# Key pages of a paged cache turned three steps ahead on VectorE, in a one-layer hybrid decoder step

## The reference

```python
q, k, v, g_a, u, v_n, g_b, m_a, m_b = split(rmsnorm(x) @ w_in)     # one projection, 5632 columns
attn = moba(q, k, v)          # prompt: causal, blocks of 256;  sample: over the cache
sgu  = u * (tril(w_s) @ v_n + b_s)                                 # chunks of 128, by group
mixed = sigmoid(m_a) * (attn * silu(g_a)) @ w_pa + sigmoid(m_b) * (sgu * silu(g_b)) @ w_pb
y = rmsnorm(x + mixed @ w_o)
# moba of the sample, for each sample, head and new position:
gate = q . mean(k over each block of 256 cached positions)         # 8 blocks
sel  = the 3 blocks with the largest gate
p    = softmax(q k / 8 + position bias, over the selected blocks and the new positions)
out  = p v
```

## Time and profile before

| | |
|---|---|
| median of 3 runs | 547.55 us (544.87 to 548.51) |
| profiled execution | 548.5 us, its span 546.7 us |
| TensorE matmuls busy | 519.2 us, 95% |
| VectorE busy | 307.8 us, 56% |
| ScalarE busy | 179.7 us, 33% |
| GpSimd busy | 121.2 us, 22% |
| granted clock of TensorE, mean | 0.986 |
| DMA | 112.00 MB, mean 205 GB/s |

### The profile page before, as it was taken

One profiled execution on the slowest core, in us unless ns is written; L12 is line 12 of the kernel. 1 busy time (PEld: TensorE's weight loads), 2 busy tenths in 40 slices (PEclk: granted clock), 3 DMA queues, 4 the chain that ended last, 5 costly groups with the idle time before them and its releaser, 6 DMA issues.

```text
span 546.7 us, 13830 instructions
## 1 busy us (share of the span) xinstructions
PE 519.2 (95%) x5624; PEld 474.6 (87%) x5624; DVE 307.8 (56%) x686; ACT 179.7 (33%) x389; POOL 121.2 (22%) x108
## 2 busy tenths in 40 slices
PE   8999999999999999999979689989979999999993
PEld 6999999989899999998979689879978999998672
DVE  6624333476765655766833767985433454784524
ACT  5522222233433432454442241212151141343313
POOL 1201111331411411321231235422360300000002
PEclk9999999999999999999999999989997999999998
DMA  8645533377648778677498998877798792360004
GB/s 253 183 155 169 182 119 119 103 229 250 195 153 272 224 252 292 200 237 247 145 334 259 302 306 285 252 245 220 255 308 292 228 330 79 126 230 1 2 10 153
DMA packets 73561, 112.00 MB, mean 205 GB/s; under 512 B 5501, under 2 KB 35338, under 8 KB 73498
## 3 DMA queue, kind: packets, MB, share of 16 engines
q1 hardware_dynamic: 72122, 107.51, 60.4%
q0 software_dynamic: 1232, 3.36, 2.1%
q10 hardware_dynamic: 144, 0.26, 0.1%
HBM read 106.57 MB, written 4.53 MB: 203 GB/s over the span
## 4 chain that ended last, share of the span: by engine, by line
PE 78%; DVE 8%; DMA 7%; SPq 3%; issue 2%; ACT 0%; POOL 0%; POOLq 0%; DVEq 0%; ACTq 0%
PE BK L583 36%; PE BK L603 9%; PE BK L922 8%; DMA KRAW<-in_cache_k 7%; PE BK L737 4%; PE BK L751 4%; PE BK L672 2%; DVE KT L1332 2%; PE BK L799 2%; PE BK L816 2%; PE BK L617 2%; PE BK L806 2%; SPq L511 1%; PE BK L852 1%; PE BK L779 1%
## 5 line engine op out<-in xcount | busy, mean ns | idle before, releaser
L583 PE MATMUL BK<-XH,WH 128*128 128x272 f32 x672 | 202.9, 302 | 0.0
L583 PE MATMUL BK<-XL,WH 128*128 128x272 f32 x672 | 194.5, 289 | 0.0
L583 PE MATMUL BK<-XH,WL 128*128 128x272 f32 x672 | 194.5, 289 | 0.0
L583 PEld LDWEIGHTS BK<-XH,WH 128*128 128x128 f32 x672 | 127.8, 190 | 10.8 <-issue 10.0
L583 PEld LDWEIGHTS BK<-XL,WH 128*128 128x128 f32 x672 | 127.7, 190 | 0.0
L583 PEld LDWEIGHTS BK<-XH,WL 128*128 128x128 f32 x672 | 127.4, 190 | 0.0
L1695 POOL TENSOR_TENSOR WL<-WRAW,WH 128x1024 fp32r<-128x1024 f32 x32 | 76.7, 2396 | 207.9 <-ACT WH L971 207.9
L1332 DVE STREAM_TRANSPOSE KT<-KRAW 128x512 f32<-128x512 f32 x128 | 87.9, 699 | 55.1 <-DMA KRAW<-in_cache_k 54.6
L971 ACT ACTIVATE WH<-WRAW 128x1024 fp32r<-128x1024 f32 x52 | 55.0, 1057 | 15.6 <-PE BK L603 15.6
L737 PE MATMUL BK<-KT,QW 128*32 128x128 f32 x1024 | 35.0, 278 | 15.5 <-DVE KT L1332 15.5
L737 PEld LDWEIGHTS BK<-KT,QW 128*32 128x32 f32 x1024 | 26.2, 110 | 20.8 <-DVE KT L1332 17.0
(11 more groups left out here) (207 smaller groups left out, 810.5 us busy)
## 6 DMA issues: line engine op xcount, KB each, us to landing
KRAW<-in_cache_k SPq DMA_DIRECT2D x128, 256.0 KB, 4.6
WRAW<-in_w_in SPq DMA_DIRECT2D x21, 1024.0 KB, 7.8
VRAW<-in_cache_v SPq DMA_DIRECT2D x56, 256.0 KB, 3.5
VQT<-in_cache_v SPq DMA_DIRECT2D x28, 256.0 KB, 4.1
VEX<-in_cache_v SPq DMA_DIRECT2D x24, 256.0 KB, 3.8
VGU<-in_cache_v SPq DMA_DIRECT2D x20, 256.0 KB, 3.7
WO<-in_w_o SPq DMA_DIRECT2D x4, 1024.0 KB, 6.3
XR<-in_x_prompt SPq DMA_DIRECT2D x4, 512.0 KB, 4.9
```

Source lines behind the costliest of these rows:

```text
L583: last = mm(BK[h][:, 0:HALF], w[:, n % 2, k, :], x[:, k, cols], start=(i == 0 and w is WH and x is XA), stop=(i == KC - 1 and w is WL))
```

## The change

VectorE turns two pages in each of the steps 0, 1 and 2, and from step 3 on page t+3 in step t; SyncE asks for page i+4 in the step in which page i is turned, as before, so its requests move along. The group x = 2 of a sample's scores used to come after `page_sums` of the groups 0 and 1 by the order of turns; it now waits for them by a semaphore of its own, `rh_ok`.

```diff
+AHEAD = 3
+def turned_at(t):
+    return [i for i in ((2 * t, 2 * t + 1) if t < AHEAD else (t + AHEAD,)) if i < PAGES]
...
 # SyncE
             for t in range(STEPS):
-                if t + KR < PAGES:
-                    load_k(t + KR)
+                for i in turned_at(t):
+                    if i + KR < PAGES:
+                        load_k(i + KR)
...
 # TensorE, page_scores
                     wait(pe, pt_ok, b - 1)
+                if x == 2:
+                    pe.wait_ge(rh_ok, b + 1)
                 for k in range(4):
...
 # VectorE, page_sums
                 peak = dve.tensor_reduce(KP[:, 4 * x:4 * x + 4], sc, AX.XY, ALU.max)
-                if x == 1:
+                if x == 0:
+                    peak.then_inc(rh_ok, 1)
+                else:
                     link(peak)
...
 # VectorE, the steps
                 if t == 0:
                     rows_out(N_QKV - 1)
-                if t < PAGES:
-                    page_turn(t)
+                for i in turned_at(t):
+                    page_turn(i)
                 if t % 4 == 0 and 4 <= t <= 128:
```

More of the change, by code:

```diff
@@ L410, in build @@
         kt_ok, sc_pe, qr_pe, qr_ok, qw_ok, bw_ok = sem("kt_ok"), sem("sc_pe"), sem("qr_pe"), sem("qr_ok"), sem("qw_ok"), sem("bw_ok")
-        r_ok, gm_pe, gm_ev, eb_ok, ex_ok = sem("r_ok"), sem("gm_pe"), sem("gm_ev"), sem("eb_ok"), sem("ex_ok")
+        rh_ok, r_ok, gm_pe, gm_ev, eb_ok, ex_ok = sem("rh_ok"), sem("r_ok"), sem("gm_pe"), sem("gm_ev"), sem("eb_ok"), sem("ex_ok")
         pt_pe, pt_ok, pl_ok, lm_pe, rl_ok = sem("pt_pe"), sem("pt_ok"), sem("pl_ok"), sem("lm_pe"), sem("rl_ok")
```

## The result

The changed kernel takes 544.15 us (median of 20 runs, 541.56 to 546.29), the kernel before 547.94 us beside it; the ratio is 0.9932, interval 0.9912 to 0.9952, or 3.8 us less. The forecast was 7.5 us less, so half of the gain is missing. The profiled execution took 545.19 us (span 543.4 us, mean granted clock 0.981).

A forecast was written before the change was run, and what follows sets the result against it. TensorE, busy 95% of the span, was taken as the bound, so only its waits for VectorE could return. Terms 3.4 - 5.3 - 3.3 + 0 + 0 - 4.6 + 2.3 = -7.5 us: profiled 541.0, median 540.0; range 532 to 548.

The forecast's parts named there:

- bank 0 at the start: Step 2: the turns of pages 4 and 5 delay the silu that frees bank 0; TensorE waits +3.4 us.
- waits of VectorE's order, and that of 3.49: Page-score waits of 1.70, 2.66 and two small ones go, -5.3 us; that of 3.49 at step 120, -3.3 us.
- waits of 3.00 and 3.67 move to the gate sums: Steps 72 and 80: these waits become one of 7.5 us for R at step 82; net 0 us.
- new waits elsewhere: Turns waiting for earlier page scores, and rh_ok at step 16b+12: taken at 0, from 0 to +2 us.
- old clock losses: After the waits at 357.25 and 411.24: 1.7 and 2.9 us lost at lower clock go, -4.6 us.
- clock behind the two new waits: After the new waits of 3.4 and 7.5 us: lower clock costs +2.3 us, between 0 and 5.8.
- each is charged the mean over the four: Each new wait costs 1.15 us of clock, the mean of 1.7, 2.9, 0 and 0 after four old waits.
- The second: Clock falls at both new waits and step 120's 3.3 us come only in half: 545 us, chance 0.27.
- its other half: Step 120: the 3.3 us come only in half, +1.7 us in the second rival, chance 0.27.
- the forecast's 536 to 545: 540.0 us with the lower and upper bounds of the start and new clock losses; chance 0.45.
- The first rival: SyncE's stretch from 287.89 moves up, so all waits go and 6.7 us come back: 532 us, chance 0.15.
- The third: VectorE stands for landings ahead of work TensorE needs at each handover; slower, 555 us, chance 0.13.

The follow-up runs named there:

- second profile: The changed kernel run again unchanged for a second profile: 542.17 us.
- the second one of before: The kernel before run again unchanged for a second profile: 550.37 us.
- the three later groups: The follow-up experiments, each group on another chip, in which the kernel before took 549.01, 550.37 and 549.11 us.
- The test with products in the waits: Changed kernel with unread products on TensorE, 7 before the wait for bank 0 and 14 before that for R: 0.9868 to the kernel before, 543.37 us.
- the lead grown late with and without the constants: Changed kernel with lead one up to step 67, three from step 70: 0.9865 to the kernel before; with constant loads also at step 80: 0.986.
- the silu moved: Changed kernel with VectorE's silu of step 2 ahead of that step's two page turns: 0.9908 to the kernel before.

## Why the prediction was half right

Term by term, on the profiled execution:

| step | forecast, us | measured, us |
|---|---|---|
| bank 0 at the start | 3.4 | 3.29, second profile 3.20 |
| waits of VectorE's order, and that of 3.49 | go | L747 waits for no turn |
| waits of 3.00 and 3.67 move to the gate sums | 7.5 | 7.21, second profile 6.57 |
| new waits elsewhere | 0 (0 to 2) | 1.23 (L809), second profile 1.35 (a bank behind ScalarE) |
| old clock losses | -4.6 | those places at 1.00 |
| clock behind the two new waits | 2.3 | 4.2 |

**The waits.** Before, L737 and L765 waited 16.9 us, and L806 0.2. The forecast takes 3.4 - 5.3 - 3.3 = -5.2 to that and so leaves 11.9; the profile has 7.8 + 3.3 + 1.2 + 0.3 = 12.6, the second one 12.5. These steps held to within 0.7 us: the prompt's wait, taken at 0, was 1.23, and the two large waits were 0.4 shorter than forecast.

**The clock is the step that failed**: "each is charged the mean over the four", 1.15 a wait. Behind the start 3.4 us at 0.50 cost 1.7. Behind the gate sums 24 projection matmuls followed each other at 0.227 us, where 0.125 is their pace at 1.00: 24 x 0.102 = 2.5. Together 4.2 instead of 2.3, and the stretch at 41.60 another 1.7. With the waits, 1.9 + 1.7 + 0.7 = 4.3, the profiled execution's distance from the forecast (545.2 against 541.0). The second profile of the changed kernel closes much the same way: 0.50 comes neither at 41.60 nor behind the start, the long wait costs 23 x 0.102 = 2.3, and its span is 6.3 us below that of the earlier trace rows, where waits and clock (-4.6 - 4.6 + 2.3) give 6.9. So one execution can come near the forecast, by luck with the clock.

Two of TensorE's projection matmuls of the changed kernel ahead of the long wait, and two behind it (starts 0.125 and 0.227 us apart):

```profile
310.62 0.29 PE L590 MATMUL BK<-XL,WH 128*128 128x272 f32 x1
310.75 0.29 PE L590 MATMUL BK<-XH,WL 128*128 128x272 f32 x1
...
319.63 0.43 PE L590 MATMUL BK<-XH,WL 128*128 128x272 f32 x1
319.86 0.43 PE L590 MATMUL BK<-XH,WH 128*128 128x272 f32 x1
```

The stretch at 41.60 belongs to that execution, not to the change: 7 of the 14 profiles have it (at 41.2 to 42.2), the second one of before among them, the second one of the changed kernel not. The mean over executions has less chance in it. The time at 0.50 is twice (1 - clock) of the span: 17.8 us in 39 executions of the kernel before in the three later groups (mean clock 0.9837), 18.9 us in 20 of the changed one (0.9826). By the forecast it should have fallen by twice 2.3 us. It didn't fall; some 4 us of it now lie within the long wait (10.20 less 6.28 busy), where they cost nothing. By these means the clock gave back some 1.5 us instead of 2.3. That and the waits explain 1.5 of the 3.7 us that are missing between the medians; the rest isn't traced, and the clocks of the kernel before in its executions beside the changed one are on record for one only (0.986). The test with products in the waits shows the price more directly: the time at 0.50 falls to some 9 us, and the ratio by 0.0064, 3.5 us, though TensorE goes on no sooner.

What was wrong in the working is the mean itself. The four waits it was taken from were of 2.7 to 3.7 us, two with a loss and two without, and four waits of one profile are too few. Over the 14 profiles of this study, from 100 us on, 0.50 stands behind 8 of 14 waits of 2 to 3 us and behind 20 of 24 of 3 to 4.4 us (it holds the end of the wait, or begins less than 2 us after it). So the wait at the start was likelier to cost its 1.7 than not. The long wait isn't of the kind that the mean was taken from: in all four profiles in which it was 6 us or more and nothing filled it (the changed kernel twice, the lead grown late with and without the constants) the stretch at 0.50 was 10.2 us long and began within the wait; at 5.5 us (the silu moved) it was 13.7. A row of that kind didn't stand in the profile of before. With four fifths of 1.7 for the start and 2.5 for the long wait, the two new waits would have been charged 3.9, an estimate from these rows, instead of 2.3.

**The rivals.** The second (545) came nearest, with the half of it that spoke of the clock; its other half, that step 120 gives back half of its gain, did not happen. The median, 544.15, lies at the upper end of the forecast's 536 to 545, which the upper bound of the clock (+3.5) had opened. The rule of the Trainium skill that it rested on (TensorE: Matmul & The Clock Gate, HAM oscillation — how this bites in real kernels: a wait for a DMA makes TensorE start the next work cold) agrees with all five waits here of 5.5 us or more, with 20 of 24 of 3 to 4.4 us and with 8 of 14 of 2 to 3 us. The first rival fell: SyncE's stretch did not move up. From 283 to 318 us SyncE waits 5.2 us for VectorE's page turns, and not once for TensorE. The third was seen in small: 1.2 us at the prompt, 1.3 to 2.5 us through ScalarE in five profiles.

**What stays open**: why the clock falls behind one short wait and not behind the next; which page is the late one near step 80, which differs from version to version; and some 2 us between the two medians.

## What to carry to other kernels

Turning ahead moves work in front of everything else in an engine's order. Where the data isn't there yet, the engine stands at the new place, ahead of work that others need; so lead by as much as the slack needs, here one step (two were no better), and not where the buffers are still filling. Many short waits that become one long one aren't a gain of their sum: price the clock behind the long one by itself. And a consumer that is moved forward takes its requests along in the issuing queue, or each of them waits behind requests that wait for the consumer's own consumer.

## What was not expected of the hardware

- Behind waits of TensorE of 2 to 4 us the granted clock fell to 0.50 in one execution and stayed at 1.00 in the next, at the same place of the same kernel: after 3.29 us at the start 0.50, after 3.20 us 1.00. Over 14 profiles 0.50 followed 8 of 14 waits of 2 to 3 us and 20 of 24 of 3 to 4.4 us.
- Unused products in the two waits raised the mean granted clock from 0.983 to 0.992, and took 3.5 us off the time by the ratios to the kernel before, 0.8 by the medians alone.
- A long wait can be followed by a long stretch at 0.50: the stretch at 314.70 began 3.3 us after TensorE had stopped (318.62 - 7.21 = 311.41) and outlasted the wait by 6.3 us.
